# Opening a third output-product block beside the last heads, and reordering the last two differential heads' projections

## The reference

```python
# differential attention, 8 heads
q, k, v = jnp.split(h @ w_in, 3, axis=-1)           # w_in: 1024 x 3072
q, k = rope_partial(q), rope_partial(k)
for i in range(T // 128):                            # query blocks of 128, causal
    p = softmax(mask(q_i @ k[:L].T))                 # two maps, m = 0 and 1
    a = p[:, :, 0] - lam * p[:, :, 1]
    out_i = a @ v[:L]
o = rmsnorm(out, subln_g) * (1 - lambda_init)
x = x + gate * (o @ w_o)                             # w_o: 1024 x 1024

# second model: y = concat(o_a, o_b) @ w_o ; x = layer_norm(alpha * x + y)
```

## Time and profile before

| | us |
|---|---|
| median of 3 runs (lowest, highest) | 1611.55 (1610.61, 1613.72) |
| the profiled execution, device time | 1609.34 |
| its span, first to last instruction | 1608.0 |
| PE busy in the span | 1540.8 |
| DVE, ACT, POOL busy | 992.7, 678.1, 194.0 |
| mean granted clock of PE, share of full | 0.985 |

### The profile page before, as it was taken

The page is one execution under the profiler, slowest core; times in us unless marked ns, Lnnn a source line. Parts: engine busy times, 40 slices in busy tenths (PEclk is TensorE's granted clock), DMA queues, the critical chain, the costliest instruction groups (busy, mean ns, idle before and its releaser), DMA issues.

```text
span 1608.0 us, 18855 instructions
## 1 busy us (share of the span) xinstructions
PE 1540.8 (96%) x7486; PEld 1252.0 (78%) x7486; DVE 992.7 (62%) x1556; ACT 678.1 (42%) x1142; POOL 194.0 (12%) x176
## 2 busy tenths in 40 slices
PE   8999999999999999999989999999999998999797
PEld 6777878888888888677758888888888867886574
DVE  7466667966666656677764644434344489896444
ACT  6444444513232335455553522323243454556533
POOL 0000002000000012111103000000002005665211
PEclk9998999999999999999989999999999999999999
DMA  9334444566656632222212443333333203112011
GB/s 372 106 114 131 136 140 154 185 207 187 206 184 205 187 117 70 70 62 66 66 40 66 121 115 99 92 96 100 92 104 100 69 27 105 54 53 67 26 53 53
DMA packets 52171, 180.78 MB, mean 112 GB/s; under 512 B 5762, under 2 KB 6658, under 8 KB 52083
## 3 DMA queue, kind: packets, MB, share of 16 engines
q1 hardware_dynamic: 52082, 179.57, 35.4%
HBM read 176.01 MB, written 3.41 MB: 112 GB/s over the span
## 4 chain that ended last, share of the span: by engine, by line
PE 82%; DVE 9%; ACT 6%; POOL 2%; issue 1%; DMA 1%; SPq 0%; DVEq 0%; ACTq 0%
PE PS L481 22%; PE PS L484 22%; PE PS L482 22%; PE PS L491 2%; PE PS L494 2%; PE PS L492 2%; DVE sb_Wl L1486 1%; PE PS L718 1%; PE PS L537 1%; PE PS L823 1%; POOL sb_TMD L2092 1%; PE PS L737 1%; PE PS L631 1%; PE PS L556 1%; ACT sb_Wh L974 1%
## 5 line engine op out<-in xcount | busy, mean ns | idle before, releaser
L481 PE MATMUL PS<-sb_Hh,sb_Wh 128*128 128x512 f32 (+1 forms) x1016 | 407.2, 401 | 2.0 <-DVE sb_Hl L1517 2.0
L484 PE MATMUL PS<-sb_Hh,sb_Wl 128*128 128x512 f32 (+1 forms) x1016 | 397.8, 392 | 0.6 <-DVE sb_Wl L1486 0.6
L482 PE MATMUL PS<-sb_Hl,sb_Wh 128*128 128x512 f32 (+1 forms) x1016 | 397.8, 392 | 0.0
L974 ACT ACTIVATE sb_Wh<-sb_RAW 128x1024 fp32r<-128x1024 f32 x223 | 233.7, 1049 | 318.9 <-PE PS L484 312.1
L1486 DVE TENSOR_TENSOR sb_Wl<-sb_RAW,sb_Wh 128x1024 fp32r<-128x1024 f32 x223 | 285.9, 1282 | 92.4 <-ACT sb_Wh L974 92.4
L481 PE MATMUL PS<-sb_Oh,sb_Wh 128*128 128x512 f32 x672 | 265.4, 395 | 1.5 <-DVE sb_Ol L1568 0.9
L482 PE MATMUL PS<-sb_Ol,sb_Wh 128*128 128x512 f32 x672 | 262.5, 391 | 0.0
L484 PE MATMUL PS<-sb_Oh,sb_Wl 128*128 128x512 f32 x672 | 262.1, 390 | 0.0
L481 PEld LDWEIGHTS PS<-sb_Hh,sb_Wh 128*128 128x128 f32 (+1 forms) x1016 | 191.1, 188 | 59.4 <-issue 16.3
L484 PEld LDWEIGHTS PS<-sb_Hh,sb_Wl 128*128 128x128 f32 (+1 forms) x1016 | 190.7, 188 | 43.3 <-DVE sb_Wl L1486 1.0
L482 PEld LDWEIGHTS PS<-sb_Hl,sb_Wh 128*128 128x128 f32 (+1 forms) x1016 | 191.2, 188 | 40.2 <-issue 1.3
(11 more groups left out here) (348 smaller groups left out, 1989.0 us busy)
## 6 DMA issues: line engine op xcount, KB each, us to landing
sb_RAW<-w SPq DMA_DIRECT2D x128, 512.0 KB, 3.6
sb_ARW<-ada SPq DMA_DIRECT2D x86, 512.0 KB, 4.4
sb_RAW<-diff_in SPq DMA_DIRECT2D x24, 512.0 KB, 3.6
sb_RAW<-gla_in SPq DMA_DIRECT2D x20, 512.0 KB, 3.7
sb_RAW<-in_b SPq DMA_DIRECT2D x16, 512.0 KB, 4.3
sb_RAW<-gla_wo SPq DMA_DIRECT2D x8, 512.0 KB, 3.6
sb_RAW<-diff_wo SPq DMA_DIRECT2D x8, 512.0 KB, 3.6
sb_RAW<-wo SPq DMA_DIRECT2D x8, 512.0 KB, 3.6
```

The source lines that it names most:

```text
L481: mm(to[0:m, :], WH[si][:, k, 0:m], hi[:, k, :], start=first, stop=False)
L482: mm(to[0:m, :], WH[si][:, k, 0:m], lo[:, k, :], start=False, stop=False)
L484: ins = mm(to[0:m, :], WL[si][:, k, 0:m], hi[:, k, :], start=False, stop=last)
L974: act(WH[slot_of(b)][:, :, 0:m], RAWS[raw_of(b)][:, 0:8 * m].rearrange("p (k m) -> p k m", k=8), ACT.Copy).then_inc(*done("w_hi", b))
```

## The change

In the differential stage the order of the projection blocks becomes: heads 0 to 5 as before, then q6, k6, q7, k7, v6, v7 (loads, projections and evacuations alike). A head's "att" task starts at the slot after its k, so head 6 stays at ticks 21 to 28 and head 7 moves from ticks 24 to 31 to ticks 23 to 30. The values of head 6 are transposed in tick 23 instead of 21. The buffer `on` of each head comes from the five TMA buffers (ring TA) instead of the thirteen of WK (ring WA).

In both output products `wo` gets a third block, in bank 4. It is opened at the third slice in the differential stage (n = 2, after tick 26) and at the second in the second model (n = 1, after tick 31), once the scores there are used; the slices already added to the first two are made up for, and from then on each slice goes into three blocks. `project` starts one block later.

```diff
+WO_THIRD = (DIFF_WO + 2, TWO_WO + 2)
-BANK = [BANKS.get(b, "turns" if b in THIRD or b in FOURTH else b % 2) for b in range(BLOCKS)]
+BANK = [BANKS.get(b, "turns" if b in THIRD or b in FOURTH else 4 if b in WO_THIRD else b % 2) for b in range(BLOCKS)]
...
+DIFF_ORDER = [(h, j) for h in range(6) for j in range(3)] + [(6, 0), (6, 1), (7, 0), (7, 1), (6, 2), (7, 2)]
+DIFF_SLOT = {k: n for n, k in enumerate(DIFF_ORDER)}
 for _h in range(8):
-    _n = 3 * _h
-    DIFF_TASKS += [(_n, "rope", (_h, 0), 1), (_n + 1, "rope", (_h, 1), 1), (_n + 2, "v", _h, 1), (_n + 2, "att", _h, 8)]
+    _q, _k, _v = (DIFF_SLOT[_h, j] for j in range(3))
+    DIFF_TASKS += [(_q, "rope", (_h, 0), 1), (_k, "rope", (_h, 1), 1), (_v, "v", _h, 1), (_k + 1, "att", _h, 8)]
...
-            def wo(first, ks, ready, tick, order=range(8)):
-                for b in (first, first + 1):
+            def wo(first, ks, ready, tick, order=range(8), third=None, free=()):
+                blocks = [first, first + 1]
+                for b in blocks:
                     open_block(b)
                 for n, k in enumerate(order[:ks]):
+                    if n == third:
+                        e.wait_ge(*(at(*f) for f in free))
+                        open_block(first + 2)
+                        blocks.append(first + 2)
+                        for m in range(n):
+                            add_k(first + 2, order[m], (Oh, Ol), m == 0, False)
                     e.wait_ge(ready(k))
-                    for b in (first, first + 1):
+                    for b in blocks:
                         add_k(b, k, (Oh, Ol), n == 0, False)
                     tick(n)
-                for b in (first, first + 1):
+                for b in blocks:
...
-            wo(DIFF_WO, 7, lambda k: at("o_lo", DIFF_WO, k), lambda n: diff_tick(25 + n))
-            for j in range(2, 7):
+            wo(DIFF_WO, 7, lambda k: at("o_lo", DIFF_WO, k), lambda n: diff_tick(25 + n), third=2,
+               free=[("d_exp", 7, 1, 1)])
+            for j in range(3, 7):
...
-            wo(TWO_WO, 7, lambda k: at("o_lo", TWO_WO, k), lambda n: two_tick(31 + n), KORDER_2)
-            for j in range(2, 8):
+            wo(TWO_WO, 7, lambda k: at("o_lo", TWO_WO, k), lambda n: two_tick(31 + n), KORDER_2, third=1,
+               free=[("a_lg", 3, i) for i in range(4)])
+            for j in range(3, 8):
...
-                        on, free_on = WA.take(("on", a), ("o_lo", DIFF_WO, a))
+                        on, free_on = TA.take(("on", a), ("o_lo", DIFF_WO, a))
```

More of the change, by code:

```diff
@@ L364, in build @@
             PLAN += [(D["w1_0"][g * 8 + c], 128) for c in range(8)] + [(D["w2_0"][g * 8 + c], 128) for c in range(8)]
-        for h in range(8):
-            PLAN += [(D["diff_in"][j], 128) for j in (h, 8 + h, 16 + h)]
+        PLAN += [(D["diff_in"][8 * j + h], 128) for h, j in DIFF_ORDER]
         PLAN += [(D["diff_wo"][j], 128) for j in range(8)]
@@ L746, in diff_tick @@
                         to, free = TB.take(("dv", a), ("d_v", a))
-                        e.wait_ge(at("evac_a", DIFF + 3 * a + 2), *free)
+                        e.wait_ge(at("evac_a", DIFF + DIFF_SLOT[a, 2]), *free)
                         turned(to, TA.buf(("dv", a))).then_inc(*done("d_vt", a))
@@ L1284, in diff_tick @@
                     elif kind == "att" and step == 7:
-                        o_hi(DIFF_WO, a, WA.buf(("on", a)), at("d_y", a))
-            for n in range(24):
-                h, j = divmod(n, 3)
+                        o_hi(DIFF_WO, a, TA.buf(("on", a)), at("d_y", a))
+            for n, (h, j) in enumerate(DIFF_ORDER):
                 if j < 2:
@@ L1826, in diff_tick @@
                         q3, free = WD.take(("q3",) + a, ("d_rope",) + a)
-                        e.wait_ge(at("evac_a", DIFF + 3 * h + j), at("sin"), *free)
+                        e.wait_ge(at("evac_a", DIFF + DIFF_SLOT[a]), at("sin"), *free)
                         e.op.stream_shuffle(q3, WA.buf(("q",) + a), ROT).then_inc(*done("d_turn", *a))
@@ L1841, in diff_tick @@
                     elif kind == "att" and step == 7:
-                        on = WA.buf(("on", a))
+                        on = TA.buf(("on", a))
                         e.wait_ge(at("d_rs", a), at("subg"))
@@ L1845, in diff_tick @@
                     elif kind == "att" and step == 8:
-                        o_lo(DIFF_WO, a, WA.buf(("on", a)))
+                        o_lo(DIFF_WO, a, TA.buf(("on", a)))
             for n in range(24):
```

## The result

The changed kernel takes 1615.33 us (median of 14 runs, 1611.37 to 1623.27) against 1609.31 (14 runs, 1604.38 to 1616.51) for the one before on the same chip: a ratio of 1.0044, 95% interval 1.0025 to 1.0062. By the ratio that is 7.1 us slower, 4.0 to 10.0; the medians themselves lie 6.0 apart. The forecast was 1616.5 and +5.0. The one of before, 1609.34, lies at its median. So the profiles show more of a difference than the medians do.

A forecast was written before the change was run, and what follows sets the result against it. PE, busy 96% of the span, was taken as the bound. Terms 1.65 + 1.9 + 1.9 = +5.4 us, or +5.0 with step 5 at the middle of its bounds, put 1611.55 at 1616.5; range 1611.0 to 1621.0.

The forecast's parts named there:

- The third block fills nothing in the second model: Second model: the block opens after tick 31, behind the 5.33 and 3.27 us waits, so its additions gain 0.
- The opening waits: Both stages: PE waits 1.9 us before the fourth block for the second's evacuation; +1.65 us in the second model.
- Rival D: Fourth-block openings cost nothing, as DVE gets to the second evacuation first: +1.7, 1613.2 us; chance 0.05.
- The clock: Behind the two new 1.9 us waits the clock holds, as after 1.67 us; nothing added, +2.0 each if it falls.
- rival C: The clock falls after both fourth-block openings: +5.0 + 4.1 = +9.1, 1620.6 us; chance 0.12.
- Step 1: DVE, differential stage: one more rope ahead of head 6's masks moves mask (6,1) from 814.73 to 816.07.
- Step 2: PE, tick 23: scores (7,3) wait for exponentials (6,1) until 818.3, idling some 4.5 us; only 2.0 us won.
- Rival B: Head 7's chain gains its tick, scores (7,3) before 814: loop -6.3, total -2.7 (-4 with clock), 1608 us; chance 0.08.
- Steps 3 and 4: Head 7: combined map (7,3) at 825.2; transpose (7,3), queued behind o_hi of head 5, at 828.1 against 827.20.
- rival A: Transpose (7,3) isn't held by o_hi of head 5, starting 2.8 us earlier: total +2.2, 1613.7 us; chance 0.2.
- Steps 5 and 6: Differential stage: transpose (7,1) at 841.6; third block ends at 858.4 (856.9 to 858.8), before 856.45: +1.9 us.
- Costs put at nothing: Loads, SP's queue, POOL's earlier products, `on` in the other ring and the third blocks' evacuations were taken as 0.

The follow-up runs named there:

- e3: The changed kernel with the fourth block of both output products in a bank of its own (bank 5): ratio 1.0012 to the kernel before.
- e11: The changed kernel with DVE evacuating the second block before splitting the fourth block's weights, in both output products: ratio 1.0017 to the kernel before.
- e7: The changed kernel with twelve small unused matmul passes on PE just ahead of the fourth block's opening in both stages: ratio 1.0035 to the kernel before.
- e1: The kernel before with the third blocks alone, opened at n = 3 in the differential stage, old order and buffers: ratio 1.0027.
- e4: The changed kernel with ACT doing tick 24's copies ahead of o_hi of head 5: ratio 1.0023 to the kernel before.
- e5: The kernel before with six slices moved ahead of ticks 24 to 26, third block after tick 27, own banks for third and fourth, differential stage: ratio 0.9953.
- e9: The kernel before with e5's edit plus additions moved ahead of the second model's two long waits: 1598.22 us, ratio 0.9934.
- e8: The kernel before with buffer `on` taken from ring TA instead of WA, nothing else: ratio 1.0002.

## Why the prediction came out as it did

The time was met, at 1615.33 for 1616.5. By the profiles the parts add to more: +5.42, +4.04 and +0.92 = 10.4 us in one execution, and 7.1 (4.0 to 10.0) in the timed median. The forecast of +5.0 lies inside that interval and was too small for the profiled execution. That the sum meets the median although it leaves out a term, the clock, is in part luck.

- **The third block fills nothing in the second model: right.** Both long waits kept their length; the cost lies behind them.
- **The opening waits: right.** 1.9 us in each stage was forecast, 2.14 and 1.86 measured, each released by the second block's residual addition behind a weight split. e3 and e11, which remove that cause in two ways, remove the wait. Rival D falls.
- **The clock: this step failed.** "So I add nothing" is wrong: in the changed kernel the clock fell behind both openings, 1.5 to 1.6 us each (e7), which the prediction had priced at 2.0 each in rival C and given 0.12. The step went by one wait, 1.67 us, and said that no wait this short costs the clock in its rows. The same trace had others that would have told it that length doesn't settle this: the clock held behind 2.26 us and fell behind 1.60 (small matmuls follow there). What came is rival C, with 3.1 us for its 4.1. The Trainium skill (TensorE: Matmul & The Clock Gate, "A second HAM failure mode: psum-queue depth-cycling") names frequent small idles between groups that cycle through banks as what makes the clock swing. These traces agree only in part: the falls came behind single waits, and the opening of e1 at 855.59, with the same 1.86 us, kept the clock. PE's timeline of before at the two waits, then the windows behind them:

```profile
127.24 0.49 PE L627 MATMUL PS<-sb_sct,sb_vT 128*128 128x128 f32 x2 [1.60 <-DVE sb_S L1633]
...
1341.42 2.15 PE L823 MATMUL PS<-sb_FB 128*128 128x128 f32 x16 [2.26 <-POOL sb_FB L2065]
```

```profile
130.00:135.00 5.00, 5.00 (x25) 5.00 (x25) 0.13 (x2) 0.00 (x0) 0.00 (x0) 0.50 0.65 204
...
1345.00:1350.00 5.00, 4.50 (x20) 3.38 (x18) 4.83 (x10) 1.06 (x2) 1.70 (x1) 1.00 0.39 107
```

- **Step 1: right in time.** Mask (6,1) at 816.19 on the clock of before, 816.07 forecast. In DVE's timeline the extra rope stands right ahead of the split and the mask (815.83 to 818.01); no run takes it away.
- **Step 2: right.** Scores (7,3) at 818.54 for 818.3, behind ACT's exponentials as said, with 3.7 us of idle for 4.5; a wait of 1.06 us ahead at 816.44 is the difference. Rival B needed them before 814, and falls; the -6.3 us of its sum don't follow from the 5.57 that it names, but nothing hangs on them.
- **Steps 3 and 4: right.** Transpose (7,3) at 828.19 for 828.1, by the series that was named; e4 shows the queue to be the cause, at 3.2 us of D for the 2.8 that separated rival A from the forecast. A falls.
- **Steps 5 and 6: right.** Transpose (7,1) at 841.69 for 841.6; the third block ends at 860.71 (its last pass starts at 860.48, and the pace is 0.23), 857.84 on the clock of before, for 858.4 (bounds 856.9 and 858.8), so +1.4 for +1.9. The 0.87 and 0.15 us are gone.
- **Costs put at nothing: one miss.** `on` in the other ring was put at 0 since no wait of PE hung on it where I looked. It costs 0.9 us in the profile, three heads earlier. The step looked for who waits for that buffer, not for what the earlier ACT would start on POOL.
- **Sum.** In D the parts close: +1.4 in the loop, 2.14 of wait, 1.6 of clock, together 5.1 for 5.42. In T: 1.86 less the gap of 0.26, and 1.5, together 3.1 of 4.04; the other 0.9 is within what T varies by from one profile to the next. The timed difference is smaller than the profiled one because the profiled execution was the second slowest of its 14 (1623.21 for a median of 1615.33). One thing that varies so from execution to execution is the clock. Behind the wait of 2.54 us ahead of head 0's scores, which every kernel has, it fell in six of the fourteen profiles, both that are compared here among them, and held in eight: 25.3 us to head 1's scores against 23.7. e5 and e9, which are the same up to there, differ in this. That the same happens at the openings, and makes up the rest of the 7.9 us, isn't shown.

## What to carry to other kernels

Independent work fills a wait of an in-order engine only if it stands ahead of that wait in the program: here a third block behind the waits was worth nothing, six slices ahead of them nothing either, and both together 5.3 us in the stage's profile, since the block supplied the work that the moved slices left missing later. Most of such a gain can be the clock rather than the idle time, so count both in the windows. When you price a wait's effect on the clock, look at every wait of that length in the trace, and give the fall a chance rather than a yes or no. Blocks that run side by side also end side by side, so the bank or buffer that the next one needs comes free late; free it before preparing the next operands, or give that block a bank of its own. Moving a transfer or a buffer "off the path" still moves when other engines start, so look for what they will run beside.

## What the runs showed of the hardware that was not expected

- The granted clock fell behind waits of 2.14 and 1.86 us that stood alone in an otherwise full stretch, and behind one of 1.60 in the kernel before; it held behind 1.67 and 2.26, and behind 1.86 in one of the two openings of e1. Behind one wait of 2.54 us it fell in six profiles and held in eight. Length alone doesn't decide it, and kernels that are the same up to a wait can go either way behind it. With twelve small matmuls in the wait it stayed at 1.00 in both openings of e7.
- A DVE addition with both inputs in SBUF took 1.64 us instead of 0.69, and a weight split 2.29 instead of 1.22, beside a POOL product of 1.3 to 1.6 us; they ended 0.55 and 1.08 us after POOL's. The Trainium skill (SBUF — State Buffer, "SBUF: two separate sides") says that whichever of the two starts first holds a shared port for its whole instruction, if DVE reads two inputs from SBUF. The e8 rows agree: POOL started at 746.45 and ended at 747.77, and the addition, begun at 746.68, ended 0.55 us after that, near its own 0.69.
